# Two transformer blocks on one Trainium2 core: the input x waits in device memory while its on-chip place holds four more buffers of weight parts, and the parts of two tiles are made by one operation

## The chip, the cores and the metric

The program runs on one core of one Trainium2 chip. The core has five engines, each with its own instruction order: TensorE (PE, matrix products), VectorE (DVE), ScalarE (ACT), GpSimd (POOL) and SyncE (SP, which here only issues transfers). They are tied together by semaphores alone: an engine waits until a counter has a value. Sixteen DMA engines move data between device memory (HBM) and the on-chip memory (SBUF, 128 partitions). The metric is the device time of one execution in microseconds (us).

## The reference, cut to what matters

Two blocks follow each other on a sequence of 256 tokens with 2048 features, all in float32. This is the part of each block that the change touches:

```
# block 1
h = rmsnorm(x, pre_mix_norm) * (1 + sc_m) + sh_m
proj = h @ w_in                      # 2048 x 8208: the "first projection"
o_hg  = hgrn2_group(proj[..., :4096])        # gated linear recurrence, 8 heads
o_gdn = gdn_group(proj[..., 4096:])          # convolution + gated delta rule, 8 heads
y = concat([o_hg, o_gdn]) @ w_out
x = x + gt_m * rmsnorm(y, post_mix_norm)     # x is needed again here
...                                          # feed-forward, then block 2:
# block 2, "mixer"
proj = u @ w_in_2                    # q, k, v of four kinds of attention
o = concat([fox, nsa, dilated, differential attention])
y = o @ w_out_2
x = x + ...                                  # and here
```

`x` itself is read before the projection (to normalize it) and after the output product (to add to it). Between those points nothing reads it.

## The kernel before

**Split products.** Each float32 operand of a product is held as two parts: the high part (a copy in the rounded type `fp32r`) and the low part (the operand less its high part). A product is then three: high by high, high by low, low by high. The parts of the activations are made once per phase. The parts of the weights are made on the way: a weight group of 512 rows comes from device memory into a ring of two groups (`core.ring`, `RING = 2`, the tile `weights`), ACT copies a tile of 128 rows into the high half of a buffer (`weight_parts`), DVE subtracts and writes the low half, and PE uses both. `w` has `KG = 4` such buffers of 128 x 2 x 512. A step of this pipeline, one weight tile, is called a *slot*.

**The first projection** (`phase_in_1`) has 256 slots, in 8 turns of 32. A group is four slots; its tiles are two rows of tiles by two chunks of 512 columns, and `place(k)` gives the order: k = 0 and 1 are the first chunk of both rows, k = 2 and 3 the second. Each slot is 12 matmuls: four with the high part alone (L1826), which wait for ACT, then eight (L1833, L1835) behind a wait for DVE. The rules of the pipeline are these:

- ACT may write buffer `slot % 4` once PE is through with slot - 4 (`core.parts_used`, L1981).
- Each half of a group (256 rows) has its own semaphore `core.landed`; ACT waits for half k at k = 0 and 1.
- DVE counts `low_ready` at k = 0 and 1 and `used` at k = 2 and 3. `used` also tells SP that half a ring slot may be loaded anew (`refill`, L104 to L117), so a half is asked for as soon as its two tiles are split.
- At slots 0 and 2 of each turn ACT, after its copy, empties the finished accumulators of the turn before (`empty`, L1855), which needs PE to be at the turn's end.

**What else runs there.** `Pace` ties other work to slots: on each engine, in program order, after the slot's own instruction. For ACT these are activations and convolution taps, for DVE the recurrence (L2056 to L2116) and the sums of the modulation, a product with the weights `w_ada` that DVE does by itself, one `L288` per slot (`pair_ada` from slot 28 on, `ada` from the third turn on). The `w_ada` loads are on SP's queue, in between the refills, and on POOL's in the second half of the first turn. At slot 22 ACT issues the load of the 16 gate columns (L1991); PE's gate products wait for it at slot 34 (semaphore `gates_in`).

**The mixer** (`phase_mixer`) has 224 slots, 14 chunks of 16 tiles, with 256 to 512 columns. Its pipeline is the same (L3187 on ACT, L3435 on DVE, L3049 on PE), with a half of a group being two tiles that follow each other. After its copy for the fourth tile of a chunk ACT empties the accumulators of the chunk before (L3088 to L3098); PE has three banks for them. The four loads of the compression weights `nsa_cmp_w1` are on ACT's queue at slots 18, 23, 28 and 33 (L3078), and PE's compression, paced at slot 40, waits for all of them. After slot 223 the last attention packs still run on PE, ACT and DVE. Between two phases there is a barrier: all engines finish one before any starts the next.

**The other products** (feed-forward, output products) already have pairs: their copy (L1149) and their subtraction (L1229) are 128 x 1024.

`x_t` (`core.xT`, 128 x 16 x 256 float32, 16 KB in each partition, 2048 KB in all) lies in SBUF for the whole program.

## Time and profile before

| | us |
|---|---|
| three runs | 2799.83, 2799.99, 2801.44 |
| their median | 2799.99 |
| the profiled execution | 2793.93 |
| its span in the trace | 2792.2 |

| stage | from, to (us of the span) | what is in it |
|---|---|---|
| setup and first turn | 0 to 140 | modulation, normalized input, slots 0 to 31 |
| first projection | 140 to 549 | slots 32 to 255; slot 48 is multiplied at 178 |
| delta rule (`phase_gdn`) | 549 to 630 | no weights of a projection |
| output product, feed-forward | 630 to 1500 | |
| mixer | 1503 to 1903 | slot 32 is split at 1562, slot 223 multiplied at 1893 |
| output product, SwiGLU, end | 1903 to 2792 | |

A row of the view by line gives the busy time of a group of instructions, the mean time of one, and how long the engine sat idle just before them, with what ended that idle time. PE's rows come in two: PEld is the load of the stationary matrix, PE the multiplication; both may show the same stall. Idle time matters where it is PE's, since PE is the engine that is hardly ever idle.

### The profile page before, as it was taken

Reading aid. Unit: us, or ns where it says so; the run is one execution under the profiler, and the core shown is the slowest. Engines: PE = TensorE matmul, PEld = TensorE weight load, DVE = VectorE, ACT = ScalarE, POOL = GpSimd, SP = SyncE. Lnnn points to the kernel's source line nnn. Section 1 sums busy time; section 2 is a strip of 40 time slices with the busy share of each in tenths; the row PEclk is TensorE's granted clock in tenths of the full one; section 3 lists DMA queues with packets and bytes.
Section 4 is the critical chain, followed back from the end, with each engine's and each line's share of the span. In section 5 each row is a group of like instructions: output and inputs, shape, how many; then the busy total and the mean of one; then the engine's idle time right before and its main releaser. Section 6 shows DMA issues by size and latency. Waiting matters only on the chain. (4 is left out here: it accounts for less than half of the span.)

```text
span 2792.2 us, 49466 instructions
## 1 busy us (share of the span) xinstructions
PE 2668.2 (96%) x18997; PEld 2383.3 (85%) x18997; DVE 1963.2 (70%) x2822; ACT 1412.5 (51%) x2328; POOL 306.2 (11%) x447
## 2 busy tenths in 40 slices
PE   7899999998999999999998999998999999999998
PEld 4679898887878888999998898887878888889998
DVE  2288996687877777898998576656787655555564
ACT  3355757645455555445444555555344444444454
POOL 1011413121011111121221010001011000000000
PEclk9999999999999999999999999999999999999999
DMA  9777676637488888898993765536578655665564
GB/s 370 296 259 238 222 234 196 210 94 244 148 286 271 280 269 272 314 334 304 328 337 127 191 194 155 150 111 221 188 267 292 223 181 180 193 185 187 176 196 133
DMA packets 290166, 632.39 MB, mean 226 GB/s; under 512 B 30722, under 2 KB 51654, under 8 KB 289734
## 3 DMA queue, kind: packets, MB, share of 16 engines
q1 hardware_dynamic: 239120, 484.78, 52.6%
q0 software_dynamic: 39424, 142.62, 14.7%
q10 hardware_dynamic: 11446, 2.54, 0.6%
q8 instruction: 122, 2.00, 0.3%
q14 instruction: 54, 0.44, 0.0%
HBM read 627.77 MB, written 2.10 MB: 226 GB/s over the span
## 5 line engine op out<-in xcount | busy, mean ns | idle before, releaser
L1149 ACT ACTIVATE weight_parts<-weights 128x1024 fp32r<-128x1024 f32 x584 | 607.3, 1057 | 583.8 <-PE accumulators L1340 248.8
L1229 DVE TENSOR_TENSOR weight_parts<-weights,weight_parts 128x1024 fp32r<-128x1024 f32 x584 | 707.8, 1222 | 271.1 <-ACT weight_parts L1149 269.4
L1329 PE MATMUL accumulators<-h_parts,weight_parts 128*128 128x512 f32 x2816 | 780.2, 399 | 22.3 <-DVE h_parts L1216 8.5
L1329 PEld LDWEIGHTS accumulators<-h_parts,weight_parts 128*128 128x128 f32 x2816 | 487.5, 191 | 92.6 <-DVE h_parts L872 10.1
L1340 PEld LDWEIGHTS accumulators<-h_parts,weight_parts 128*128 128x128 f32 x2944 | 454.4, 191 | 72.2 <-DVE weight_parts L1229 10.7
L1340 PE MATMUL accumulators<-h_parts,weight_parts 128*128 128x256 f32 x2944 | 475.1, 283 | 7.7 <-DVE weight_parts L1229 7.7
L1833 PE MATMUL accumulators<-in_h_parts,in_weight_parts 128*128 128x256 f32 x1024 | 264.4, 290 | 20.5 <-DVE in_weight_parts L2142 20.1
L2142 DVE TENSOR_TENSOR in_weight_parts<-weights,in_weight_parts 128x512 fp32r<-128x512 f32 x256 | 186.6, 748 | 110.4 <-ACT in_weight_parts L1983 109.6
L1835 PE MATMUL accumulators<-in_h_parts,in_weight_parts 128*128 128x256 f32 x1024 | 260.7, 286 | 0.0
L1373 PE MATMUL accumulators<-h_parts,weight_parts 128*128 128x512 f32 x864 | 236.5, 395 | 2.0 <-issue 1.8
L1983 ACT ACTIVATE in_weight_parts<-weights 128x512 fp32r<-128x512 f32 x256 | 154.8, 627 | 146.9 <-PE accumulators L1835 101.7
L1833 PEld LDWEIGHTS accumulators<-in_h_parts,in_weight_parts 128*128 128x128 f32 x1024 | 199.4, 195 | 26.4 <-DVE in_weight_parts L2142 25.9
L3049 PE MATMUL accumulators<-in_h_parts,in_weight_parts 128*128 128x256 f32 x1632 | 213.8, 286 | 5.5 <-ACT wide L3098 3.1
L1393 PE MATMUL accumulators<-h_parts,weight_parts 128*128 128x256 f32 x864 | 216.8, 283 | 0.2 <-DVE weight_parts L1229 0.2
L1395 PE MATMUL accumulators<-h_parts,weight_parts 128*128 128x256 f32 x864 | 216.6, 283 | 0.0
L3049 PEld LDWEIGHTS accumulators<-in_h_parts,in_weight_parts 128*128 128x128 f32 x1632 | 201.6, 191 | 15.7 <-issue 8.5
L3435 DVE TENSOR_TENSOR in_weight_parts<-weights,in_weight_parts 128x512 fp32r<-128x512 f32 (+6 forms) x224 | 130.0, 596 | 118.8 <-ACT in_weight_parts L3187 116.9
L1835 PEld LDWEIGHTS accumulators<-in_h_parts,in_weight_parts 128*128 128x128 f32 x1024 | 199.8, 195 | 0.0
L3187 ACT ACTIVATE in_weight_parts<-weights 128x512 fp32r<-128x512 f32 (+6 forms) x224 | 121.2, 554 | 144.7 <-PE accumulators L3049 138.3
L1826 PE MATMUL accumulators<-in_h_parts,in_weight_parts 128*128 128x256 f32 x1024 | 177.7, 296 | 12.7 <-DVE in_h_parts L1661 8.7
L1826 PEld LDWEIGHTS accumulators<-in_h_parts,in_weight_parts 128*128 128x128 f32 x1024 | 142.7, 193 | 41.0 <-issue 22.5
L1373 PEld LDWEIGHTS accumulators<-h_parts,weight_parts 128*128 128x128 f32 x864 | 147.7, 189 | 22.6 <-issue 2.1
(418 smaller groups left out, 3624.7 us busy)
## 6 DMA issues: line engine op xcount, KB each, us to landing
weights<-in_w_ff SPq DMA_DIRECT2D x256, 512.0 KB, 6.0
weights<-in_w_in SPq DMA_DIRECT2D x160, 512.0 KB, 5.3
wide<-in_w_ada SPq DMA_DIRECT2D x112, 512.0 KB, 10.3
h_t<-in_ada_w POOLq DMA_DIRECT2D x112, 512.0 KB, 6.8
weights<-in_ffn_w_gate SPq DMA_DIRECT2D x88, 512.0 KB, 4.5
weights<-in_ffn_w_up SPq DMA_DIRECT2D x88, 512.0 KB, 4.5
weights<-in_ffn_w_down SPq DMA_DIRECT2D x88, 512.0 KB, 4.1
weights<-in_w_out SPq DMA_DIRECT2D x64, 512.0 KB, 5.4
```

The costliest lines, as they stand in the source:

```text
L1149: nc.scalar.activation(w[:, held:held + take, 0, :], core.ring[:, q % RING, k:k + take, :], ACT.Copy).then_inc(core.high_ready, take)
L1229: ins = nc.vector.tensor_tensor(w[:, held:held + take, 1, :], core.ring[:, q % RING, k:k + take, :], w[:, held:held + take, 0, :].bitcast( ...
L1329: nc.tensor.matmul(both(nt), high, x[:, kt].rearrange("p a t -> p (a t)"), start=(kt == 0), stop=False, skip_group_check=True)
L1340: ins = nc.tensor.matmul(rest(nt) if two else acc(c, nt), w[:, held, 1, nt * P:(nt + 1) * P], x[:, kt, 0, :], start=False, stop=(kt == KT ...
L1373: nc.tensor.matmul(both(nt), w[:, held, 0, cols[nt]], xk.rearrange("p a t -> p (a t)"), start=first, stop=False, skip_group_check=True)
L1393: nc.tensor.matmul(accs[nt], w[:, held, 0, cols[nt]], xk[:, 1, :], start=False, stop=False, skip_group_check=True)
L1395: ins = nc.tensor.matmul(accs[nt], w[:, held, 1, cols[nt]], xk[:, 0, :], start=False, stop=(last and nt % 2 == 1), skip_group_check=True)
L1826: nc.tensor.matmul(acc(c, nt), w[:, k, 0, nt * P:(nt + 1) * P], x[:, kt, 0, :], start=(kt == 0 and nt % 2 == 0), stop=False, skip_group_ch ...
L1833: nc.tensor.matmul(acc(c, nt), w[:, k, 0, nt * P:(nt + 1) * P], x[:, kt, 1, :], start=False, stop=False, skip_group_check=True)
L1835: ins = nc.tensor.matmul(acc(c, nt), w[:, k, 1, nt * P:(nt + 1) * P], x[:, kt, 0, :], start=False, stop=(kt == KT - 1 and nt % 2 == 1), sk ...
L2142: ins = nc.vector.tensor_tensor(w[:, k, 1, :], core.ring[:, g % RING, part, :], w[:, k, 0, :].bitcast(F32), ALU.subtract)
L3049: ins = nc.tensor.matmul(out, stationary[:, a], moving[:, b], start=(kt == 0 and i == 0 and j == 0), stop=(kt == KT - 1 and i == 2 and j = ...
```

## The change

The change has four parts.

1. **Pairs.** From slot 48 of the first projection (`DEEP_SLOT`) and slot 32 of the mixer (`MIX_DEEP_SLOT`) on, ACT makes the high parts of two tiles in one operation of 128 x 1024, and DVE the low parts likewise. In the first projection a pair is k = 0, 1 or k = 2, 3: one tile of each half of the group, so ACT waits for both halves before the first pair, and both counts of `used` come with the second pair. In the mixer a pair is a half of a group.
2. **Four more buffers.** From the same slots on, the buffers are eight: the four of `w` and four (`w_in_x`) at the address of `x_t`. ACT waits for PE to be through with slot - 8, of the pair's second tile.
3. **x in device memory.** ACT issues a store of all of `x_t` (2048 KB) to `x_kept` at slot 26 of the first projection and at slot 20 of the mixer. ACT waits for the store's end before it first writes `w_in_x` (slot 52, slot 36). SP loads `x_t` back in the delta-rule phase, and in the mixer after the last matmul that uses a weight part; each of the two phases ends only when that load has landed.
4. **One semaphore** (`gates_in_x_moved`) counts the gate columns and the moves of x. PE's gate products at slot 34 now wait for 32, which is the gate columns and the store of x.

```diff
+X_KEPT_SLOT, DEEP_SLOT = 26, 48
...
+        w_in_x = nc.alloc_sbuf_tensor_at("in_1_weight_parts_in_x", [P, KG, 2, CW], F32R, offset=core.x_at)
...
+        def parts(slot):
+
+            if slot < DEEP_SLOT:
+                return w, slot % KG
+            return (w, slot % (2 * KG)) if slot % (2 * KG) < KG else (w_in_x, slot % (2 * KG) - KG)
+
+        def parts_free(act, slot):
+
+            if DEEP_SLOT + KG <= slot < DEEP_SLOT + 2 * KG:
+                act.wait_ge(core.gates_in_x_moved, 32)
+            elif slot >= KG:
+                act.wait_ge(core.parts_used, slot + 1 - (KG if slot < DEEP_SLOT + KG else 2 * KG))
...
-                pe.wait_ge(s["gates_in"], 16)
+                pe.wait_ge(core.gates_in_x_moved, 32)
...
+                elif k % 2 == 0:
+                    if k == 0:
+                        for half in range(HALVES):
+                            act.wait_ge(core.landed[g % RING][half], 16 * ((st.first + g) // RING + 1))
+                    parts_free(act, slot + 1)
+                    nc.scalar.activation(held[:, at:at + 2, 0, :], core.ring[:, g % RING, part::2, :], ACT.Copy
+                                         ).then_inc(core.high_ready, 2)
...
+                if slot == X_KEPT_SLOT:
+                    act.dma_start(core.x_kept, core.xT[:].rearrange("p a b -> p (a b)")).then_inc(core.gates_in_x_moved, 16)
...
+                elif k % 2 == 0:
+                    dve.wait_ge(core.high_ready, slot + 2)
+                    nc.vector.tensor_tensor(held[:, at:at + 2, 1, :], core.ring[:, g % RING, part::2, :],
+                                            held[:, at:at + 2, 0, :].bitcast(F32), ALU.subtract
+                                            ).then_inc(core.used if k >= 2 else core.low_ready, 2)
...
+        @block.sync
+        def _(sp):
+            sp.dma_start(core.xT[:].rearrange("p a b -> p (a b)"), core.x_kept).then_inc(core.gates_in_x_moved, 16)
+            sp.wait_ge(core.gates_in_x_moved, 48)
...
+MIX_KEPT_SLOT, MIX_DEEP_SLOT = 20, 32
...
             prefetch(sp, core, core.streams["out_2"])
+            sp.wait_ge(core.parts_used, row_tile(0, SLOTS))
+            sp.dma_start(core.xT[:].rearrange("p a b -> p (a b)"), core.x_kept).then_inc(core.gates_in_x_moved, 16)
+            sp.wait_ge(core.gates_in_x_moved, 80)
...
+                    elif k % 2 == 0:
+                        if MIX_DEEP_SLOT + KG <= slot < MIX_DEEP_SLOT + 2 * KG:
+                            act.wait_ge(core.gates_in_x_moved, 64)
+                        else:
+                            back = KG if slot < MIX_DEEP_SLOT + KG else 2 * KG
+                            act.wait_ge(core.parts_used, row_tile(c, kt) + 2 - back)
+                        nc.scalar.activation(held[:, at:at + 2, 0, 0:width], core.ring[:, g % RING, k:k + 2, 0:width],
+                                             ACT.Copy).then_inc(core.high_ready, 2)
```

**DVE, slots 183 to 188 of the first projection.** L2142 (L2175 after) is the subtraction that makes the low parts, L288, L293, L299 and L302 are the modulation's sums, L2080, L2056 and L2061 (L2106, L2082, L2087) the recurrence. Before:

```order
L2142 TENSOR_TENSOR in_1_weight_parts<-weights,in_1_weight_parts 128x512 x2
L288 SCALAR_TENSOR_TENSOR turn_sums<-wide,c_act,turn_sums 128x512
L2056 TENSOR_TENSOR scaled<-h_t 128x1024
L2142 TENSOR_TENSOR in_1_weight_parts<-weights,in_1_weight_parts 128x512
L288 SCALAR_TENSOR_TENSOR turn_sums<-wide,c_act,turn_sums 128x512
L293 TENSOR_TENSOR turn_sums<-turn_sums 128x512
L299 STREAM_TRANSPOSE turn_sums<-turn_sums 128x512
L302 TENSOR_REDUCE modulation<-turn_sums 128x16
L2080 COPY_PREDICATED attn_t<-up_mask,accumulators 64x8x16x2 x2
L2061 TENSOR_TENSOR scaled<-h_t 128x1024
L2142 TENSOR_TENSOR in_1_weight_parts<-weights,in_1_weight_parts 128x512 x5
```

After:

```order
L2175 TENSOR_TENSOR in_1_weight_parts_in_x_49<-weights,in_1_weight_parts_in_x_49 128x2x512
L288 SCALAR_TENSOR_TENSOR turn_sums<-wide,c_act,turn_sums 128x512
L2082 TENSOR_TENSOR scaled<-h_t 128x1024
L2175 TENSOR_TENSOR in_1_weight_parts<-weights,in_1_weight_parts 128x2x512
L288 SCALAR_TENSOR_TENSOR turn_sums<-wide,c_act,turn_sums 128x512
L293 TENSOR_TENSOR turn_sums<-turn_sums 128x512
L299 STREAM_TRANSPOSE turn_sums<-turn_sums 128x512
L302 TENSOR_REDUCE modulation<-turn_sums 128x16
L2106 COPY_PREDICATED attn_t<-up_mask,accumulators 64x8x16x2 x2
L2087 TENSOR_TENSOR scaled<-h_t 128x1024
L2175 TENSOR_TENSOR in_1_weight_parts<-weights,in_1_weight_parts 128x2x512
```

The low part of slot 185 now comes with that of slot 184, ahead of the long run of other work instead of behind it.

**ACT, slots 22 to 28 of the first projection.** L1983 (L2000) is the copy that makes the high parts, L1991 (L2015) the load of the gate columns. Before:

```order
L1991 DMA w_gates<-in_w_in 128x16x16
L1983 ACTIVATE in_1_weight_parts<-weights 128x512 [waits parts_used]
L432 ACTIVATE h_t<-h_t,modulation,affine 128x256 [waits input_factored,input_normalized]
L432 ACTIVATE h_t<-h_t,modulation,affine 128x256 x3
L1656 ACTIVATE in_1_h_parts<-h_t 128x4x256 [waits scalar_steps]
L1983 ACTIVATE in_1_weight_parts<-weights 128x512 [waits parts_used,weights_landed_0_half_0]
L1983 ACTIVATE in_1_weight_parts<-weights 128x512 [waits parts_used,weights_landed_0_half_1]
L1983 ACTIVATE in_1_weight_parts<-weights 128x512 [waits parts_used] x2
L1983 ACTIVATE in_1_weight_parts<-weights 128x512 [waits parts_used,weights_landed_1_half_0]
```

After:

```order
L2015 DMA w_gates<-in_w_in 128x16x16
L2000 ACTIVATE in_1_weight_parts<-weights 128x512 [waits parts_used]
L432 ACTIVATE h_t<-h_t,modulation,affine 128x256 [waits input_factored,input_normalized]
L432 ACTIVATE h_t<-h_t,modulation,affine 128x256 x3
L1658 ACTIVATE in_1_h_parts<-h_t 128x4x256 [waits scalar_steps]
L2000 ACTIVATE in_1_weight_parts<-weights 128x512 [waits parts_used,weights_landed_0_half_0]
L2000 ACTIVATE in_1_weight_parts<-weights 128x512 [waits parts_used,weights_landed_0_half_1]
L2000 ACTIVATE in_1_weight_parts<-weights 128x512 [waits parts_used]
L2018 DMA x_kept<-x_t 128x4096
L2000 ACTIVATE in_1_weight_parts<-weights 128x512 [waits parts_used]
L2000 ACTIVATE in_1_weight_parts<-weights 128x512 [waits parts_used,weights_landed_1_half_0]
```

The store of x stands four copies behind the gate load in the same queue, ahead of the copies of slots 27 and 28.

**SP, the end of the mixer.** The rows are the transfers of the mixer's last weights and of the next product's first ones. Before and after in one piece:

```order
 L117 DMA weights<-in_w_in 128x2x256 x16
 L117 DMA weights<-in_w_out 128x2x512 x4
-L2841 UNCONDITIONAL_BRANCH
+L2924 DMA x_t<-x_kept 128x4096
+L2880 UNCONDITIONAL_BRANCH
```

The load of x is the last thing on SP's queue in the mixer, and the branch to the next phase stands behind it.

## Rows read from the trace of the kernel before

**Rows 1.** The page: busy time of each engine, share of the span, count.
```profile
PE 2668.2 (96%) x18997; PEld 2383.3 (85%) x18997; DVE 1963.2 (70%) x2822; ACT 1412.5 (51%) x2328; POOL 306.2 (11%) x447
```

**Rows 2.** Waits, 178 to 549 us: who waited for whom, total, times, longest.
```profile
PE accumulators L1833 <- DVE in_weight_parts L2142: 18.5, 17, 2.1
...
PEld accumulators L1833 <- DVE in_weight_parts L2142: 24.0, 25, 2.3
...
ACT in_weight_parts L1983 <- PE accumulators L1835: 91.9, 92, 3.7
ACT in_weight_parts L1983 <- DMA weights<-in_w_in: 27.9, 19, 4.1
...
DVE in_weight_parts L2142 <- ACT in_weight_parts L1983: 56.3, 44, 4.3
```

**Rows 3.** Busy time by stretch: length, engines, TensorE clock, DMA share, GB/s.
```profile
178.00:275.00 97.00, 93.61 (x773) 90.53 (x773) 81.64 (x131) 55.15 (x98) 7.87 (x9) 1.00 0.70 226
275.00:297.00 22.00, 19.71 (x144) 18.70 (x143) 22.00 (x25) 14.95 (x29) 15.18 (x12) 0.92 0.69 251
...
326.00:352.00 26.00, 22.00 (x222) 20.99 (x221) 25.64 (x30) 19.12 (x36) 16.39 (x17) 1.00 0.61 207
352.00:402.00 50.00, 48.30 (x482) 47.04 (x482) 44.65 (x66) 31.39 (x51) 5.96 (x7) 1.00 0.77 248
402.00:430.00 28.00, 24.50 (x226) 23.22 (x222) 24.68 (x31) 16.77 (x32) 7.84 (x8) 1.00 0.59 195
...
504.00:527.00 23.00, 20.21 (x157) 18.92 (x156) 22.91 (x30) 15.21 (x20) 0.00 (x0) 1.00 0.65 228
527.00:549.00 22.00, 20.35 (x181) 19.80 (x179) 13.35 (x23) 7.94 (x17) 0.00 (x0) 1.00 0.64 218
```

**Rows 4.** DVE's timeline around slot 185: start, duration, instruction, idle before.
```profile
410.70 0.69 DVE L2142 TENSOR_TENSOR in_weight_parts<-weights,in_weight_parts 128x512 fp32r<-128x512 f32 x1
...
416.94 1.29 DVE L2142 TENSOR_TENSOR in_weight_parts<-weights,in_weight_parts 128x512 fp32r<-128x512 f32 x2
```

**Rows 5.** DVE's timeline at the start of the output product, pairs back to back.
```profile
1905.28 2.35 DVE L1229 TENSOR_TENSOR weight_parts<-weights,weight_parts 128x1024 fp32r<-128x1024 f32 x2
```

**Rows 6.** DMA issues, 178 to 549 us: KB each, median us from issue to landing.
```profile
weights<-in_w_in SPq DMA_DIRECT2D x100, 512.0 KB, 5.3
```

**Rows 7.** ACT's and DVE's timelines, slots 22 to 30.
```profile
115.89 0.40 ACTq L1991 DMA_DIRECT2D w_gates<-in_w_in  x1
...
123.38 2.18 ACT L1983 ACTIVATE in_weight_parts<-weights 128x512 fp32r<-128x512 f32 x4
...
140.03 0.49 DVE L284 TENSOR_SCALAR turn_sums<-wide,c_act 128x512 f32<-128x512 f32 x1 [3.44 <-DMA wide<-in_w_ada]
```

**Rows 8.** Busy time by stretch (as rows 3), and a DMA issue (as rows 6).
```profile
131.00:149.00 18.00, 12.96 (x94) 12.46 (x93) 9.21 (x16) 7.65 (x17) 2.17 (x3) 0.91 0.92 335
...
w_gates<-in_w_in ACTq DMA_DIRECT2D x1, 128.0 KB, 18.0
wide<-in_x SPq DMA_DIRECT2D x1, 2048.0 KB, 7.9
```

**Rows 9.** Waits of PE in the mixer, 1562 to 1894 us (as rows 2).
```profile
PE accumulators L3049 <- DVE in_weight_parts L3435: 5.3, 6, 1.7
PE accumulators L3049 <- ACT wide L3098: 3.8, 5, 1.5
```

**Rows 10.** The mixer's last load on ACT's queue, PE's first use, DMA meanwhile.
```profile
1563.48 0.60 ACTq L3078 DMA_DIRECT2D h_t<-in_nsa_cmp_w  x1
...
1579.29 0.54 PE L2898 MATMUL accumulators<-wide,h_t 128*64 128x30 f32 x12
...
1547.00:1563.00 16.00, 15.40 (x126) 15.28 (x127) 7.44 (x16) 9.29 (x23) 0.00 (x0) 1.00 1.08 243
```

**Rows 11.** PE's timeline at the mixer's end.
```profile
1892.84 0.52 PE L3049 MATMUL accumulators<-in_weight_parts,in_h_parts 128*128 128x256 f32 x3
...
1899.11 2.88 PE L3020 MATMUL accumulators<-maps_t,wide 128*128 128x256 f32 x16 [0.80 <-ACT maps_t L3167]
```

77 lines of the change are left out of this document (51 added, 26 removed).

## The prediction

> **What bounds the kernel now.** I read the page first: PE is busy 96% of the span [rows 1], so only idle time of PE can be won, or matmuls taken away, and the change takes none away. Next came PE's waits where the change works. From slot 48 of the first projection to its end (178 to 549 us) PE waits for DVE's low parts: 18.5 us on the row of the multiplications, 24.0 us on that of the weight loads; these are two views of the same stalls, and the loss lies between [rows 2]. In the mixer it is 5.3 us for low parts and 3.8 us for the emptying of accumulators by ACT [rows 9]. Last, the busy time by stretch, to see why. PE's idle time is the length less PE's busy time: 3.4, 2.3, 4.0, 1.7, 3.5, 2.8 and 1.7 us in the seven stretches of [rows 3], 19.4 us in all. Where it is densest, DVE is busy without a break (22.00 of 22, 25.64 of 26, 22.91 of 23 us). Elsewhere it has time left: over the whole stage it idles 56.3 us waiting for ACT's high parts, and ACT idles 91.9 us waiting for PE to free a buffer [rows 2]. So DVE isn't short of time on average (305.9 of 371 us). It is short of buffers in which to work ahead before a burst of other work. One burst is plain: from 410.70 to 416.94 us DVE makes no low part, since 6 us of modulation sums and recurrence stand between those of slots 184 and 185 [rows 4].
>
> **Part 1, deeper buffers, first projection.** 208 slots take 371 us, 1.8 us each. With four buffers DVE can be ahead by four slots less a copy and a subtraction (0.6 and 0.7 us [rows 4, 7]): 5.9 us at best, 4.5 where slots are short. With eight and pairs it is seven slots less a pair's copy and subtraction (some 1 and 1.2 us [rows 5]), 10 us at best. A burst of 6 us then fits. It fits only if the lead has been earned: DVE must have had idle time first, and at each turn's end ACT must wait for PE's last slots to empty accumulators, which cuts the lead to three slots eight times, in both kernels. So I go by stretch, with DVE's idle time there [rows 3]: 178 to 275 has 15.4 us of it, I take 3.0 of 3.4; 275 to 297 none, 1.2 of 2.3; 326 to 352, 0.4 us, 2.0 of 4.0; 352 to 402, 1.0 of 1.7; 402 to 430, 2.5 of 3.5 (the plain burst, whole, and half of the rest); 504 to 527, 1.2 of 2.8 (it follows a turn's end); 527 to 549, 0.8 of 1.7. That is 11.7 us. In 275 to 297 the granted clock was 0.92, so part of it ran at the lower level, 1.2 GHz instead of 2.4; 0.08 of 22 us is 1.8 us, and it came after PE had stood still. If the stall is half gone I count 0.8 us of that. Sum 12.5 us. The bounds are 3 us (only the first stretch) and 24.0 + 1.8 us.
>
> **Part 2, pairs.** A pair costs 2.35 / 2 = 1.18 us on DVE [rows 5], two singles back to back 1.29 us [rows 4]: 0.11 us saved, 104 times, 11 us of DVE's time. Off the critical path it is worth nothing; in the three stretches without idle time (71 of 371 us, 20 pairs) it is 2.2 us, which is in the sum above. The Trainium skill, "VectorE: DVE Perf Modes", section on the TRN2 errata, says that an operation from SBUF pays a fixed extra latency, about 151 cycles at 0.96 GHz for a float32 subtraction of this kind. By that rule a pair saves 0.16 us, and the dense stretches 3.2 us; the rows of this trace, where operations follow each other without a gap, show less, and I go by them. The price of pairs is in the ring of weights, and it is the first rival.
>
> **Part 3, the mixer.** The same reasoning for its 5.3 us: its bursts are short and its slots too; I take 3.5 us. The 3.8 us is another thing: ACT empties a chunk's accumulators behind its fourth copy, which with four buffers may only start once PE is through with the old chunk. With eight the copy is done before, so the emptying starts one copy (about 0.6 us) earlier; at five recorded waits that is up to 3 us, I take 2.5. Sum 6 us, bounds 1 and 9.1 us.
>
> **Part 4, storing x.** In the first projection the store comes at slot 26. ACT makes the copies of slots 24 to 27 from 123.38 us on, so it is issued at about 125 us, on the queue whose gate load was issued at 115.89 us and took 18.0 us, to 133.9 us [rows 7, 8]. I assume that the store's data follow that. They then fall into 131 to 149 us, when the DMA engines are busy 0.92 of the time at 335 GB/s and PE only 12.96 of 18 us [rows 8]: PE hangs on transfers there, and DVE waits 3.44 us for a `w_ada` load [rows 7]. 2.1 MB at 335 GB/s are 6.3 us. If all of it goes ahead of what PE needs, PE loses 6.3 us; if it goes between, nothing. PE's gate products at slot 34 (about 148 us) now also wait for the store. Shared with two other queues at a third of the rate the store takes 6.3 x 3 = 19 us, to 153 us, but PE will be late by then itself. The delays overlap, so I take 3.5 us for both; bounds 0 and 6.3. What is queued on PE behind the gates' wait is slot 35's matmuls, so the wait is paid in full if it occurs. In the mixer the store goes between the first and second of four loads for the compression. The last of these is issued at 1563.48 us, PE first uses them at 1579.29 us, and DMA is at 1.08 meanwhile [rows 10]. A delay of up to 2.1 MB / 243 GB/s = 8.6 us falls on a cover of 15.8 us less a landing of some 6 to 10 us. I take 1.5 us, bounds 0 and 8.6. Both issues on ACT (0.4 to 0.6 us each, by the other loads there) are covered by its lead.
>
> **Part 5, loading x back.** In the delta-rule phase it is issued first and has 81 us; nothing there waits for it, so nothing, as long as it lands within the phase. At the mixer's end it decides: it starts when the last weight matmul is over (1893.4 us), a 2048 KB load took 7.9 us [rows 8], so it lands at 1901.3 us; the mixer's last matmul ends at 1902.0 us [rows 11]. The cover is 0.7 us. The first weights of the output product stand ahead in the same queue; if 1 MB of them is still on the way, 3.1 us at 335 GB/s come on top: 2.4 us late. I take 1.0, bounds 0 and 2.4.
>
> **The sum.** 12.5 + 6 - 3.5 - 1.5 - 1.0 = 12.5 us less. From the profiled execution's 2793.93 us that gives 2781.4; the median of the runs is 6.06 us above it, so 2787.5 us. I say **2787 us**.
>
> **Rivals.** *The ring of weights takes the place of the buffers.* It still holds two groups. In the first projection both halves are now given back with the second pair, and both must have landed before the first copy. Between DVE's end of one group and its start on the next but one lies one group of work, 4 x 1.8 = 7.1 us; needed are 5.3 us of landing [rows 6] and a copy of 1 us, 6.3 us. On average it fits, with 0.8 us to spare; where slots are 1.5 us it doesn't (6.0 us), and ACT has waited 27.9 us for weights already [rows 2]. Then the lead is never earned and part 1 gives 4 us instead of 12.5: 2796 us. *DMA time decides (slower).* Store and load cost their bounds, 6.3 + 8.6 + 2.4 = 17.3 us, and the weights come later too, so that parts 1 and 3 give 4 + 6. That is 7 us more: 2807 us. It decides from the point at which x costs more than the 10 us left. For it speaks DMA at 0.92 and 1.08 just where the stores fall, against it the 0.6 to 0.7 in most of [rows 3]. "DMA: Bandwidth & Descriptors" in the Trainium skill, section on issuing engines, says that transfers from all queues end on the same 16 engines and interleave. By that x's own queue buys nothing, which leans to this rival; no row here has three queues at once. *Nearly all stalls go.* The lead of ten microseconds covers every burst: 19.4 + 1.8 + 9.1 - 6 = 24 us less, 2776 us. For it speaks that no single recorded stall is longer than 2.1 us [rows 2], against it the turns' ends.
>
> **How the numbers follow.** Forecast 0.55 (own range 2780 to 2794), ring 0.20, DMA 0.10, nearly all 0.15. About 0.2%, 5.6 us, is what a measurement can tell from no change. Faster by more than that (under 2794.4) are the forecast, nearly all, and a tenth of the ring's case: 0.72. Slower (over 2805.6): 0.11. The same: 0.17. The range holds the forecast, the ring's case and most of nearly all, and leaves out DMA and the best cases: 2770 to 2803.
>
> **What would show it.** In the profile after, PE's wait for DVE's low parts in the first projection should fall from 18.5 to about 7 us, and DVE should still be without a break in the dense stretches. If ACT's wait for weights rises well over 27.9 us and its wait for PE falls to little, it was the ring. If slot 48 is multiplied more than 5 us later than at 178 us, or the mixer's last phase ends behind x's landing, it was DMA. A new wait of PE at the gate or compression products shows part 4. The prediction is wrong if the lead of DVE doesn't grow past four slots, or if the moves of x cost over 10 us.

## The result: slower by 0.6%

The changed kernel takes 2813.72 us (median of 10 runs, 2807.65 to 2822.76); the kernel before, run beside it, takes 2798.84 us (10 runs, 2790.51 to 2802.09). The ratio is 1.0061, with a 95% interval of 1.0049 to 1.0073: slower by 15 to 17 us, where 12.5 us less were forecast, and outside the range. The profiled execution after is the slowest of its ten, 2822.76 us with a span of 2820.8 us, and the profiled execution before (2793.93 us) is one of the shorter ones. The two traces are therefore 28.8 us apart where the medians are 14.9 apart: the sizes of whole kernels are taken from the medians, and the traces say where the time goes, in sizes that run too high in all.

Where the time goes is read by laying the two traces over each other: for each slot of the first projection the start of its first matmul after, less that before, and for the mixer the same at every 96th matmul. The lag in us:

```
first projection, slot   0    28    32    48    64    112   160   208   255
after - before         +1.5  +1.4  +8.2  +8.2  +6.9 +13.0 +15.9 +23.4 +27.4
mixer, at (before)      1521  1565  1594  1664  1743  1893 us
after - before         +31.6 +32.4 +34.7 +32.1 +31.6 +28.4
```

There are three pieces: a step of 6.8 us between slots 28 and 32, a growth of 19.3 us from slot 48 to 255, and in the mixer a step of 3.3 us followed by a gain of 6.3 us. The 4.2 us between the two stages are put down to the execution and not to the change; in the runs below that same stretch varies from -7 to +6 us.

**The growth behind slot 48.** The waits of the changed kernel from 178 to 570 us, beside [rows 2] (engine, tile and line, who released it, total us, times, longest):

```profile
ACT in_weight_parts L2007 <- DMA weights<-in_w_in: 52.2, 12, 8.4
DVE in_weight_parts L2175 <- ACT in_weight_parts L2007: 48.4, 22, 5.7
ACT in_weight_parts_in_x L2007 <- DMA weights<-in_w_in: 46.0, 12, 6.7
DVE in_weight_parts_in_x L2175 <- ACT in_weight_parts_in_x L2007: 43.0, 20, 3.5
...
ACT in_weight_parts L2007 <- PE accumulators L1851: 20.2, 5, 6.1
...
PE accumulators L1849 <- DVE in_weight_parts_in_x L2175: 11.1, 13, 1.8
PE accumulators L1849 <- DVE in_weight_parts L2175: 11.0, 10, 3.1
...
ACT in_weight_parts_in_x L2007 <- PE accumulators L1851: 4.9, 3, 2.5
```

Each wait now stands on two rows, for the old and the new buffers. ACT's wait for PE's buffers fell from 91.9 to 25.1 us, as the deeper buffers promise, but its wait for weights rose from 27.9 to 98.2 us, and DVE's wait for ACT from 56.3 to 91.4 us. PE's wait for DVE went from 18.5 to 22.1 us instead of to 7. The same in the dense stretches (busy time in each window; length, PE, PEld, DVE, ACT, POOL, TensorE clock, DMA share, GB/s):

```profile
285.00:308.00 23.00, 18.25 (x143) 17.14 (x142) 18.74 (x19) 14.20 (x23) 13.71 (x12) 1.00 0.63 223
337.00:365.00 28.00, 22.03 (x190) 20.66 (x189) 24.05 (x24) 18.71 (x30) 16.73 (x16) 0.97 0.56 189
```

DVE, which had no break there [rows 3], now idles 4.3 of 23 and 4.0 of 28 us, and PE stands still for 4.8 and 6.0 us, longer than before. The DMA engines are busy only 0.56 to 0.63 of the time, so it isn't their bandwidth: the weights are asked for too late (which runs without the coupling, below, bear out).

**The step at slot 32.** DVE's timeline after, beside [rows 7] (start, duration, line, in brackets idle before and its releaser), the same window as [rows 8], and the transfers from 120 to 150 us (KB each, median us to landing):

```profile
146.28 0.49 DVE L284 TENSOR_SCALAR turn_sums<-wide,c_act 128x512 f32<-128x512 f32 x1 [8.30 <-DMA wide<-in_w_ada]
...
131.00:149.00 18.00, 8.37 (x46) 7.39 (x45) 3.15 (x6) 3.25 (x7) 0.72 (x1) 0.78 0.85 344
...
wide<-in_w_ada POOLq DMA_DIRECT2D x5, 512.0 KB, 22.2
weights<-in_w_in SPq DMA_DIRECT2D x4, 512.0 KB, 17.9
x_kept<-x_t ACTq DMA_DIRECT2D x1, 2048.0 KB, 22.0
```

DVE waits 8.30 us for the first modulation load where it waited 3.44. It works in order, so its next low parts wait behind that sum; PE is busy 8.37 us of 18 instead of 12.96, and the granted clock falls from 0.91 to 0.78. The new wait of PE for the store, at the gate products, costs nothing: the lag is 8.2 us at slot 32 and at slot 48, the store has landed at 146.0 us, and the first gate product starts at 157.7 us.

### The profile page after: what moved, and what is told of

It is laid out like the page before. It is cut to its first block and busy times, and to the rows that moved or that the text cites. A ratio compares the mean times of both kernels' runs of the same rounds, so it can differ in the third digit from the quotient of the medians.

```text
span 2820.8 us, 49227 instructions
## 1 busy us (share of the span) xinstructions
PE 2677.9 (95%) x18997; PEld 2389.4 (85%) x18997; DVE 1936.5 (69%) x2622; ACT 1375.0 (49%) x2128; POOL 310.9 (11%) x447
## 5 line engine op out<-in xcount | busy, mean ns | idle before, releaser
L1329 PEld LDWEIGHTS accumulators<-h_parts,weight_parts 128*128 128x128 f32 x2816 | 486.1, 191 | 96.2 <-DVE h_parts L872 10.1
L1340 PEld LDWEIGHTS accumulators<-h_parts,weight_parts 128*128 128x128 f32 x2944 | 453.2, 190 | 70.3 <-DVE weight_parts L1229 10.1
L1340 PE MATMUL accumulators<-h_parts,weight_parts 128*128 128x256 f32 x2944 | 473.7, 283 | 6.7 <-DVE weight_parts L1229 6.5
L1393 PE MATMUL accumulators<-h_parts,weight_parts 128*128 128x256 f32 x864 | 216.7, 283 | 0.4 <-DVE weight_parts L1229 0.4
L1395 PE MATMUL accumulators<-h_parts,weight_parts 128*128 128x256 f32 x864 | 216.6, 283 | 0.0
L1849 PE MATMUL accumulators<-in_h_parts,in_weight_parts 128*128 128x256 f32 x608 | 163.1, 298 | 17.2 <-DVE in_weight_parts L2175 11.0
L1373 PEld LDWEIGHTS accumulators<-h_parts,weight_parts 128*128 128x128 f32 x864 | 147.7, 189 | 23.4 <-issue 2.1
L1393 PEld LDWEIGHTS accumulators<-h_parts,weight_parts 128*128 128x128 f32 x864 | 165.9, 192 | 0.6 <-DVE weight_parts L1229 0.6
L1395 PEld LDWEIGHTS accumulators<-h_parts,weight_parts 128*128 128x128 f32 x864 | 165.9, 192 | 0.0
L288 DVE SCALAR_TENSOR_TENSOR ada_sums<-h_t,c_act,ada_sums 128x512 f32<-128x512 f32 x224 | 159.9, 746 | 3.1 <-DMA h_t<-in_ada_w 2.8
L1851 PE MATMUL accumulators<-in_h_parts,in_weight_parts 128*128 128x256 f32 x608 | 160.9, 294 | 0.0
L238 POOL DMA_DIRECT2D h_t<-in_ada_w x112 | 80.5, 719 | 724.3 <-DVE ada_sums L288 237.7
L1376 PEld LDWEIGHTS accumulators<-h_parts,weight_parts 128*128 128x128 f32 x864 | 132.5, 189 | 18.4
L1849 PEld LDWEIGHTS accumulators<-in_h_parts,in_weight_parts 128*128 128x128 f32 x608 | 123.1, 203 | 20.4 <-DVE in_weight_parts L2175 13.7
L1389 PE MATMUL accumulators<-h_parts,weight_parts 128*128 128x256 f32 x864 | 138.9, 283 | 0.0
L1148 ACT ACTIVATE h_parts<-wide 128x512 fp32r<-128x512 f32 x108 | 68.6, 636 | 141.3 <-DMA weights<-in_w_ff 59.6
L1376 PE MATMUL accumulators<-h_parts,weight_parts 128*128 128x256 f32 x864 | 137.4, 281 | 0.0
L1842 PE MATMUL accumulators<-in_h_parts,in_weight_parts 128*128 128x256 f32 x608 | 108.7, 302 | 18.2 <-DVE in_h_parts L1663 10.0
```

The source lines that it names most:

```text
L288: ins = nc.vector.scalar_tensor_tensor(out=acc, in0=w, scalar=number, in1=acc, op0=ALU.mult, op1=ALU.add)
L1329: nc.tensor.matmul(both(nt), high, x[:, kt].rearrange("p a t -> p (a t)"), start=(kt == 0), stop=False, skip_group_check=True)
L1340: ins = nc.tensor.matmul(rest(nt) if two else acc(c, nt), w[:, held, 1, nt * P:(nt + 1) * P], x[:, kt, 0, :], start=False, stop=(kt == KT ...
L1373: nc.tensor.matmul(both(nt), w[:, held, 0, cols[nt]], xk.rearrange("p a t -> p (a t)"), start=first, stop=False, skip_group_check=True)
L1376: ins = nc.tensor.matmul(rest(nt), w[:, held, 1, cols[nt]], xk[:, 0, :], start=False, stop=last, skip_group_check=True)
L1389: nc.tensor.matmul(accs[nt], w[:, held, 0, cols[nt]], xk[:, 0, :], start=(first and nt % 2 == 0), stop=False, skip_group_check=True)
```

## The experiments

Two theories about the growth were put against each other: **A**, the ring of weights is coupled (a pair takes one tile of either half, so both halves are wanted at the first copy and given back at the last), and **C**, operations of two tiles cost by themselves. **B** puts the whole loss on the moves of x. All medians below are beside 2795.56 us for the kernel before (19 to 22 runs beside them), those of before_light, deep_light, mixer_only and late_mix_pairs beside 2795.13 us (31 runs), and the last two beside 2795.78 us (17 runs).

**x_moves_only**: the change without its buffers and pairs, in both stages (the diff is the first projection's).

```diff
-            if slot < DEEP_SLOT:
+            if True:
                 return w, slot % KG
...
-                if slot < DEEP_SLOT:
+                if True:
                     if k < HALVES:
```

> The two stores and two loads of x and the shared semaphore of the change, and nothing else of it: four buffers and one tile per operation, as before. Theory A (from slot 48 on the pairs, which take a tile of each half of a group, hold both halves until the second pair and want both before the first copy, so that the weights in the ring become the limit; the store of x costs about 7 us at slots 30 to 40, the other moves 2 to 4): 2806 to 2811 us where the kernel before has 2799, that is +7 to +12, with the whole loss of the first projection in place by slot 48. Theory B (the store and the loads of x are the whole slowdown, by what they do to later transfers): +15 to +17, with the lag still growing after slot 48. Theory C (operations of two tiles are the cost by themselves): as A.

Measured: 2806.95 us, ratio 1.0038 (1.0027 to 1.0050), +11.4 us. The lag steps by 6.5 us at slot 32, stays at 6.7 until slot 136, ends at 8.9, and steps by 2.9 us in the mixer at 1577 us. So the moves of x cost 11 us by themselves, all but 2 us of the traced part in two steps; B falls as the whole, since the growth behind slot 48 is missing.

**deep_single**: the change, eight buffers and moves of x, with one tile per operation.

```diff
-                if slot < DEEP_SLOT:
+                if True:
                     if k < HALVES:
                         act.wait_ge(core.landed[g % RING][k], 16 * ((st.first + g) // RING + 1))
```

> The changed kernel with one tile per operation in both stages; the eight buffers and the moves of x stay. Theory A: the halves of a group are again wanted and given back one at a time, so the lag behind the kernel before stops growing at slot 48 and the deeper buffers win some of it back: 2794 to 2806 us (-5 to +7). Theory B (moves of x): as the changed kernel, +15. Theory C (operations of two tiles cost by themselves): as A. Theory D (eight buffers themselves are harmful, because refills are asked for in other places and collide): +10 or more, with growing lag.

Measured: 2794.73 us, ratio 0.9996 (0.9986 to 1.0005). The pairs are therefore worth some 16 to 19 us of loss (each kernel's median beside its own kernel before gives 15.7 us, the ratios 1.0061 and 0.9996, 0.65% apart, give 18.2 us, the two medians 19.0 us; the intervals leave 4 us to either side), as much as the whole slowdown. From 178 to 570 us ACT's waits read:

```profile
ACT in_weight_parts L2000 <- DMA weights<-in_w_in: 46.1, 24, 5.8
ACT in_weight_parts_in_x L2000 <- DMA weights<-in_w_in: 37.0, 21, 4.6
...
PE accumulators L1849 <- DVE in_weight_parts L2170: 12.9, 11, 2.1
...
PE accumulators L1849 <- DVE in_weight_parts_in_x L2170: 7.0, 9, 1.4
```

Here too ACT waits for weights (83.1 us) in place of buffers, but PE's wait for DVE is 19.9 us, as it was. The first projection from slot 48 to 255 loses 0.8 us in this trace and gains nothing. Against x_moves_only the kernel is 12.2 us faster by the medians and 8.2 us by the two profiled executions; the traces place 1.5 us of that in the first projection and 5.3 us by the mixer's end, and more runs below were made to tell whether the first projection has a share.

**pairs_four**: pairs as in the change, four buffers, no move of x.

```diff
-            if slot < DEEP_SLOT:
+            if True:
                 return w, slot % KG
...
-                if slot == X_KEPT_SLOT:
-                    act.dma_start(core.x_kept, core.xT[:].rearrange("p a b -> p (a b)")).then_inc(core.gates_in_x_moved, 16)
```

> Operations of two tiles as in the change, with four buffers only and without any move of x. Theory A: the ring coupled, and no depth: the lag grows from slot 48 by at least the 19 us that the changed kernel loses there, and perhaps by twice that as TensorE now waits for pairs: +20 to +45 us in all, ScalarE waiting over 70 us for weights in the first projection. Theory B (moves of x): no change or a gain, -5 to +3. Theory C: as A.

Measured: 2840.82 us, ratio 1.0157 (1.0133 to 1.0181), +45 us, at the upper end of A's range. The lag is 0 at slot 48, 30.7 us at slot 255, and grows by 15.9 us through the mixer, where a pair lies in one half and nothing is coupled. With four buffers, then, pairs have a second cost: only two operations' worth of buffers are left, and ACT waits 127.1 us for PE (91.9 before). The deep buffers pay for that part. ScalarE's wait for weights, though, is 31.9 us and not the 70 that A had named: with four buffers the longer wait is that for buffers.

**halves_coupled**: the kernel before, single tiles, four buffers, and only the coupling, from slot 48 on (so the second hunk too).

```diff
-                if k < HALVES:
-                    act.wait_ge(core.landed[g % RING][k], 16 * ((st.first + g) // RING + 1))
+                if k == 0:
+                    for half in range(HALVES if slot >= 48 else 1):
+                        act.wait_ge(core.landed[g % RING][half], 16 * ((st.first + g) // RING + 1))
...
-                ins.then_inc(core.used if k >= 2 else core.low_ready, 1)
+                ins.then_inc(core.used if k == 3 else core.low_ready, 2 if k == 3 else 1)
```

> The kernel before with one tile per operation and four buffers, but from slot 48 of the first projection on ScalarE waits for both halves of a group ahead of its first copy and VectorE gives both back after its fourth remainder. Nothing else. This is the coupling alone. Theory A: +12 to +30 us, all of it in the first projection behind slot 48, ScalarE's waits for weights going from 28 us to over 70. Theory C (it is the two-tile operations themselves, not the coupling): within 4 us of the kernel before. Theory B: the same.

Measured: 2808.78 us, ratio 1.0049 (1.0032 to 1.0066), +13.2 us, and in the trace 14.1 us from slot 48 to 255. ACT's row, beside 27.9 in [rows 2]:

```profile
ACT in_weight_parts L1988 <- DMA weights<-in_w_in: 78.5, 28, 5.4
ACT in_weight_parts L1988 <- PE accumulators L1837: 51.1, 48, 5.1
```

No operation has changed its size here; the coupling alone costs 13 us (n is four; the interval leaves 9 to 18). It has two parts, the wait for both halves and their late return, and no run tells these apart.

**deep_coupled**: deep_single with that same coupling, so that only its size of operation differs from the change.

```diff
+                    if k == 0:
+                        for half in range(HALVES if slot >= DEEP_SLOT else 1):
+                            act.wait_ge(core.landed[g % RING][half], 16 * ((st.first + g) // RING + 1))
...
-                                            ).then_inc(core.used if k >= 2 else core.low_ready, 1)
+                                            ).then_inc(core.used if k == 3 else core.low_ready, 2 if k == 3 else 1)
```

> One tile per operation, eight buffers and the moves of x (the kernel deep_single, 2795 us), and from slot 48 of the first projection on both halves of a group awaited at its first copy and given back with its fourth remainder. Theory A (the coupling of the halves is what the two-tile operations cost): most of the 17 us that lie between deep_single and the changed kernel, +11 to +18 over deep_single: 2806 to 2813 us, with ScalarE's waits for weights near the 98 us of the changed kernel. Theory C (the size of the operations costs, since TensorE can start only when both tiles are copied and subtracted): within 4 us of deep_single, 2791 to 2799.

Measured: 2810.97 us, ratio 1.0052 (1.0036 to 1.0069), 16.2 us over deep_single; slot 48 to 255 grows by 15.5 us (19.3 in the changed kernel). ACT idles 112 us ahead of its copies from 178 to 570 us (A had said near 98), though its rows name no releaser there. A holds; the remainder of some 2 us is within what the intervals leave open.

**rows_pairs**: the change with its pairs inside one half of a group, that is the two chunks of one row tile.

```diff
-        return k // 2, k % 2, 2 * (k % 2) + k // 2
+        if slot >= DEEP_SLOT:
+            return k % 2, k // 2, k
+        return k // 2, k % 2, 2 * (k % 2) + k // 2
...
-                        for half in range(HALVES):
-                            act.wait_ge(core.landed[g % RING][half], 16 * ((st.first + g) // RING + 1))
+                    act.wait_ge(core.landed[g % RING][k // 2], 16 * ((st.first + g) // RING + 1))
```

> The changed kernel with its two-tile operations, but from slot 48 of the first projection on in the other order: a pair is the two tiles of one half (the two chunks of one row tile), awaits that half alone and gives it back at once; the second chunk's accumulators are emptied a slot earlier to fit. Theory A: the 17 us over deep_single go, and with fewer operations perhaps 1 to 3 us more: 2790 to 2798 us. Theory C (size of the operations): 2808 to 2814, as the changed kernel.

Measured: 2803.15 us, ratio 1.0033 (1.0020 to 1.0047): 8 us over deep_single, and by the ratios 0.28% or 8 us under the change. Neither theory's range holds it. Undoing the coupling gives back half. The other half is lost from slot 48 to 255 (8.4 us in the trace). Three things stayed or came with the new order: the size of the operations, the emptying of the second chunk at another slot, and SP's queue. A half is now given back a slot or two sooner, but modulation loads that wait for DVE stand ahead of its refill (SP's waits from 178 to 550 us):

```profile
SPq L238 <- DVE turn_sums L288: 159.3, 42, 8.2
SPq L117 <- DVE in_weight_parts L2179: 83.1, 26, 9.8
SPq L117 <- DVE in_weight_parts_in_x L2179: 57.5, 28, 4.7
```

Summed over the 104 refills of that part, 129 us pass between DVE's last low part of a half and the issue of its refill, 24 us in deep_single. The last two kernels below were made to tell the three apart.

**deep_late**: deep_single with both stores of x moved. The store in the first projection also waits on ACT for the gate columns to have landed, PE's gate products no longer wait for it, and the mixer's deep buffers start at slot 56.

```diff
-X_KEPT_SLOT, DEEP_SLOT = 26, 48
+X_KEPT_SLOT, DEEP_SLOT = 36, 48
...
-MIX_KEPT_SLOT, MIX_DEEP_SLOT = 20, 32
+MIX_KEPT_SLOT, MIX_DEEP_SLOT = 42, 56
...
-                pe.wait_ge(core.gates_in_x_moved, 32)
+                pe.wait_ge(core.gates_in_x_moved, 16)
```

> deep_single (2795 us) with both stores of x moved: in the first projection from slot 26 to slot 36, behind the chip's last use of the modulation loads of slots 28 to 32, and the gate columns' product waiting for its own load alone; in the mixer from slot 20 to slot 42, behind the loads of W1, with the deep buffers from slot 56 instead of 32. Theory E (a store at slot 26 and 20 costs what it does because it collides with loads that somebody is about to want: 6.7 and 2.9 us in the traces): 2785 to 2789 us. Theory F (2 MB cost their DMA time wherever they stand): within 3 us of deep_single, 2792 to 2798.

Measured: 2790.27 us, ratio 0.9982 (0.9972 to 0.9991), 4.5 us under deep_single and 5.3 us under the kernel before. Both steps are gone: the lag is 1.3 and 1.2 us at slots 28 and 32 (0.2 and 6.5 in deep_single), and in the mixer -1.88 us at 1565 and at 1594 us. The window of [rows 8] and the store, issued at 148.7 us, read:

```profile
131.00:149.00 18.00, 12.96 (x93) 12.27 (x93) 8.01 (x14) 7.29 (x17) 1.83 (x3) 0.90 0.85 305
...
x_kept<-x_t ACTq DMA_DIRECT2D x1, 2048.0 KB, 10.6
```

PE's 12.96 us are back to the digit, and the store lands in 10.6 instead of 22.0 us. E holds: the place of the store costs, not its bytes. (That PE's gate products no longer wait for the store can't be the reason, since deep_single's step lies ahead of slot 34.) The time is a microsecond above E's range.

**rows_late**: rows_pairs and the moved stores together.

> rows_pairs and the moved stores of deep_late together. Theories A and E: 2781 to 2788 us, faster than both kernels. If A holds and F instead of E: 2790 to 2798. If C holds: over 2800 whichever of E and F does.

Measured: 2793.78 us, ratio 0.9987 (0.9977 to 0.9997), 3.5 us over deep_late. The moved stores give 9.4 us here, the two traced steps together; the trace still grows by 7.7 us from slot 48 to 255. The time lies in none of the ranges for A and E together (up to 2788) or for C (over 2800); it is in the one for F, but deep_late has ruled F out.

**before_light** and **deep_light**: the kernel before, and deep_late, with refills that bring half of the columns.

```diff
+        if stream is core.streams["in_1"] and stream.unit * i + q >= 14:
+            cols = cols // 2
+        sp.dma_start(ring[:, slot, at, 0:cols], src[:, at, 0:cols]).then_inc(core.landed[slot][half], 16)
```

> The kernel before with the refills of the first projection from group 14 on (slot 56) bringing half of each tile's columns only; the other half of the columns in the ring is what lay there, so this leaves out half of the weights' transfers and no work of the engines. It asks what weights that land sooner are worth with four buffers. Theory G (with four buffers ScalarE waits for the buffers that TensorE gives back, 92 us against 28 us for weights, so sooner weights do little): 0 to -4 us, 2791 to 2796.

> deep_late (eight buffers, one tile per operation, stores of x moved; 2790 us) with the same half-sized refills from group 14 of the first projection on. Theory G (with eight buffers the ring of weights has taken the buffers' place, ScalarE waiting 88 us for weights): the lead is now earned, -8 to -15 us against deep_late: 2775 to 2782, and ScalarE's waits for weights fall under 30 us. Theory H (VectorE's own work in the dense stretches is the limit, and earlier weights only move waits about): within 3 us of deep_late, 2787 to 2793.

Measured: before_light 2792.76 us, ratio 0.9990 (0.9981 to 0.9999), deep_light 2789.36 us, ratio 0.9980 (0.9970 to 0.9989). The refill of deep_light lands in 3.6 us instead of 5.0:

```profile
weights<-in_w_in SPq DMA_DIRECT2D x70, 256.0 KB, 3.6
```

and yet it is only 0.9 us under deep_late. G falls and H's range holds: once the halves are uncoupled, weights that land sooner buy next to nothing. ACT's wait for them falls from 88.1 to 60.7 us (G had it under 30), so the ring isn't out of play yet, and a longer ring wasn't tried; but those 27 us less bought 0.9. How full the buffers really were answers why. Counted in the traces, for each of the 208 slots from 48 on: how many slots' low parts were ready when PE started the slot, its own included (0 means that its own isn't ready yet).

```
kernel        mean ready   slots with 0 / 1 / 2 / 3 / 4 / 5 ready
before           1.35        48 / 71 / 57 / 32 /  0 /  0
deep_late        1.54        48 / 67 / 45 / 32 / 13 /  3
deep_light       1.70        48 / 62 / 39 / 29 / 23 /  7
after            1.68        34 / 71 / 59 / 24 / 11 /  9
```

With four buffers DVE stood at its limit of three in 32 slots of 208, and in 48 it had nothing ready. With eight those 48 are still 48, and 42 of them are the same slots, slot 185 behind the plain burst of [rows 4] among them. They come in 23 runs in the kernel before; only in 1 of these had the buffers been full within the four slots ahead, and in 7 within eight. The buffers were full just where they weren't needed. (In the changed kernel PE finds its slot unready less often, 34 times, and yet loses more: its longest recorded wait for low parts is 3.1 us instead of 2.1, and it now waits 4.6 us for high parts, 0.6 before.)

**mixer_only**: the first projection as before, the change in the mixer with the store at slot 42 and deep buffers from slot 56. **late_mix_pairs**: deep_late with the change's pairs in the mixer.

```diff
-MIX_KEPT_SLOT, MIX_DEEP_SLOT = 20, 32
+MIX_KEPT_SLOT, MIX_DEEP_SLOT = 42, 56
...
-                if slot < DEEP_SLOT:
+                if True:
                     if k < HALVES:
```

> The first projection as in the kernel before; in the attention stage the change's eight buffers and two-tile operations, with the store of x at slot 42 and the deep buffers from slot 56. If the first projection's part brings nothing even with its store moved, and the mixer's part 3.5 to 4.5 us as in the traces of deep_late and rows_late: 2790 to 2793 us where the kernel before has 2795.6, that is -3 to -5. If the first projection's deep buffers bring something of their own, this is worse than deep_late (2790) by that much.

> deep_late with the change's two-tile operations in the attention stage, where a pair lies in one half of a group. From the traces a pair there wins 0.7 (rows_late against deep_late) to 2.8 us (the changed kernel against deep_single): 2787.5 to 2789.5 us. If operations of two tiles cost by themselves there too: over 2791.

Measured: mixer_only 2790.07 us, ratio 0.9982 (0.9971 to 0.9992); late_mix_pairs 2789.44 us, ratio 0.9978 (0.9969 to 0.9987), the fastest of those that load all of the weights and 5.7 us under the kernel before. From the mixer's 480th matmul to its end the lag changes by -5.7 and -5.6 us in the two, by -3.6 in deep_late with single tiles. The mixer's part is therefore the whole gain as far as these runs can tell, and the eight buffers of the first projection are worth nothing that they show: late_mix_pairs has them and mixer_only hasn't, and the intervals of the two leave 3 us of loss to 5 us of gain. That pairs beat single tiles in the mixer is what most traces show (by some 2 us, in rows_late by 0.7 only); the medians (0.8 us) can't tell it.

**rows_single**: rows_late with one tile per operation in the first projection, its order of slots kept.

```diff
-                    nc.scalar.activation(held[:, at:at + 2, 0, :], core.ring[:, g % RING, part:part + 2, :], ACT.Copy
-                                         ).then_inc(core.high_ready, 2)
+                    nc.scalar.activation(held[:, at, 0, :], core.ring[:, g % RING, part, :], ACT.Copy
+                                         ).then_inc(core.high_ready, 1)
```

> rows_late (2793.8 us) with one tile per operation in the first projection, but its order of slots (both chunks of a row tile, a half given back with its second tile) and its earlier emptying of the second chunk kept. If the size of the operations is what rows_late loses against deep_late (2790.3), this comes out as deep_late with pairs in the mixer, 2788.5 to 2791 us, and the 7.7 us of growth from slot 48 to 255 go. If the order of the slots, the queue of refills or the emptying is the cause: 2793 to 2796 us, with the growth kept.

Measured: 2797.98 us, ratio 1.0006 (0.9997 to 1.0015). The growth from slot 48 to 255 is still there, 7.8 us, with no operation of two tiles left in that stage, so the size of the operations isn't what rows_late and rows_pairs lose; if anything it wins (0.9987 against 1.0006, intervals that just touch). C falls. The loss comes with the order of the slots. It isn't SP's queue either as far as this run goes, since the 104 refills are 61.5 us late in sum here and 129 in rows_late, with the same growth. In rows_late and rows_single it comes in steps, one of the largest (3.0 and 3.5 us) right behind slot 64, where a turn starts and the first accumulators are emptied at the new slots. PE waits there for that emptying, 2.1 us in rows_late and 2.6 in rows_single, a wait that deep_late lacks:

```profile
PE accumulators L1844 <- ACT wide L1877: 3.6, 2, 2.6
```

That is rows_single from 178 to 570 us; in rows_late the same row is 2.5 us. So the emptying accounts for a third to a half of the 7.8 us, and the rest stays open.

**rows_loads_later**: rows_late with each modulation load one refill later in the queue.

```diff
-AFTER_REFILL = {2: (2, 3), 3: (4,), 4: (5,), 5: (6, 7), 6: (8,), 7: (9,)}
-BEHIND_PAIR = {7: (8, 9)}
+AFTER_REFILL = {0: (1,), 3: (2, 3), 4: (4,), 5: (5,), 6: (6, 7), 7: (8,)}
+BEHIND_PAIR = {7: (8,)}
```

> rows_late with the first projection's modulation loads issued one refill later in the queue that they share with the refills, so that fewer refills stand behind a load that waits for VectorE. If the queue is the cause: 2787 to 2791 us and the 129 us summed over 104 refills between a half's return and the issue of its refill fall under 60. If the size of the operations is the cause: within 2 us of rows_late, 2792 to 2796, whatever the refills do.

Measured: 2828.46 us, ratio 1.0108 (1.0090 to 1.0126), 35 us over rows_late, which neither expectation had. The refills did what was meant, 5.9 us late in the sum of 104 instead of 129. But the modulation loads have no slack either:

```profile
DVE turn_sums L288 <- DMA wide<-in_w_ada: 49.4, 20, 4.5
```

In [rows 2] no such wait is among the large ones. DVE works in order, so the low parts behind each such sum wait too, and the queue's order is already a compromise between the two. What refills in time are worth by themselves this run can't tell.

## Why the prediction was wrong, point by point

**What bounds the kernel.** Right as to the rows, wrong in the reading "it is short of buffers in which to work ahead". The evidence was ACT's wait of 91.9 us for PE to free a buffer. That wait says that ACT was far ahead, not that DVE was held up: in 32 of 208 slots DVE had filled what there was, and only 1 of the 23 runs of unready slots came within four slots of such a place. The stalls fall where DVE had been behind for longer, and buffers that DVE hasn't filled before are no help there.

**Part 1, deeper buffers, first projection (12.5 us).** This is one of the two steps that failed; the other, the larger, is the price of the pairs in part 2. The text named its condition, "only if the lead has been earned", and then counted DVE's idle time in a stretch as earned lead. Measured without the pairs: 0.8 us lost in deep_single, 0.4 gained in deep_late, and 2.5 with weights that land in 3.6 us. All of these are within what executions differ by: mixer_only, whose first projection is that of the kernel before, loses 3.1 us in the same stretch. So the 12.5 us became nothing that the runs can tell, at most some 5. With the change's pairs it is 19.3 us lost in the trace. The lower bound of 3 us was no bound either: a loss had been left out. The sign named for a wrong prediction, a lead that doesn't grow past four slots, nearly came: five slots were ready in 3 of 208 slots in deep_late and in 9 in the changed kernel, never more, where seven had been counted on.

**Part 2, pairs, and the first rival.** The mechanism was named exactly: both halves wanted before the first copy and given back with the second pair. ACT's wait for weights "well over 27.9 us" with little wait for PE was the sign given, and it came (98.2 and 25.1 us). Its size was wrong: 6.3 us needed against 7.1 us there "on average" was taken to fit, leaving 4 us of gain (2796 us). An average of 0.8 us to spare isn't slack when slots, averaged over eight, take from 1.4 us (168 to 176) to 2.5 us (208 to 216) in the kernel before. That a group that comes late also delays its own return, and so the next group but one, is the likely reason for the size and not shown. The coupling costs 13.2 us with four buffers and 16.2 with eight. In the sum the pairs' price stood at nothing, and it is this term, not part 1, that turned no gain into a loss: with parts 1 and 2 at nothing and the rest as measured the kernel would be about 5 us slower, not 15. That pairs are worth nothing "off the critical path" was right; they are worth less than nothing where they tie two transfers together. Their size alone does no harm (rows_single).

**Part 3, the mixer (6 us).** Right in the sum: from 1594 us to its end the changed kernel gains 6.3 us, rows_pairs 6.3, late_mix_pairs 5.6. The two terms behind it were off in opposite directions, though. PE's waits behind the store, from 1597 to 1894 us before (the first two rows; that for the low parts is the first of [rows 9]) and from 1631 to 1923 us after (the other four), where L3088 and L3098 (L3138 and L3148) are the emptying:

```profile
PE accumulators L3049 <- ACT wide L3098: 3.2, 4, 1.5
PE accumulators L3049 <- ACT wide L3088: 1.2, 2, 0.8
...
PE accumulators L3099 <- DVE in_weight_parts L3506: 2.9, 2, 1.7
PE accumulators L3099 <- DVE in_weight_parts_in_x L3506: 1.1, 1, 1.1
PE accumulators L3099 <- ACT wide L3148: 0.3, 1, 0.3
PE accumulators L3099 <- ACT wide L3138: 0.2, 1, 0.2
```

The low parts' 5.3 us fell by 1.3 and not by 3.5, and in deep_late they didn't fall at all (5.3 us from 1594 to 1888 us); the emptying gave 3.9 us and not 2.5. The last microsecond of the 6.3 is on none of these rows. So here too the lead brought little, and it was luck that the other term made up for it.

**Part 4, the stores (3.5 and 1.5 us).** The place and the way were right, the sizes too small. The first cost 6.8 us (6.5 in x_moves_only), above the upper bound of 6.3. That bound was the store's own bytes at 335 GB/s; it left out that DVE waits in order, so that one late modulation load stops the low parts too, and that PE, once still, runs on at a lower clock (0.78 for 0.91). The store doesn't merely follow the gate load on its own queue: the modulation loads and the refills land late with it, 22.2 and 17.9 us after their issue. Nor did it take "a third of the rate". The queues from 137 to 142 us of the changed kernel (q10 is ACT's, q0 POOL's, q1 SP's: packets, MB, share of the 16 DMA engines' time):

```profile
q10 hardware_dynamic: 88, 1.44, 67.7%
q0 software_dynamic: 87, 0.36, 17.3%
q1 hardware_dynamic: 90, 0.33, 16.0%
```

The three queues get equally many packets, but one of the store's is 16 KB (a row of `x_t` in a partition) and one of the others 4 KB or less, so the store takes two thirds of the bytes while DVE waits for a load on q0. The second cost 3.3 us against 1.5, inside its bounds. It stands in the same trouble, beside the compression's loads and refills that land in 8.5 us instead of 7.1 (transfers issued from 1575 to 1600 us; 7.1 is that of 1545 to 1570 us before; no landing recorded for the second row):

```profile
weights<-in_w_in SPq DMA_DIRECT2D x5, 512.0 KB, 8.5
h_t<-in_nsa_cmp_w ACTq DMA_DIRECT2D x4, 512.0 KB
x_kept<-x_t ACTq DMA_DIRECT2D x1, 2048.0 KB, 10.0
```

By "DMA: Bandwidth & Descriptors" in the Trainium skill, section on issuing engines, transfers of all queues end on the same 16 engines and interleave; the trace now shows three queues at once and agrees, with 373 to 486 GB/s in all from 134.25 to 147 us and packets of all three in turn.

**Part 5, loading back (0 and 1.0 us).** Right. The first load, issued at 577.5 us, lands in 8.4 us, within its phase, and nothing waits for it. The second is issued at 1921.8 us; its landing (first row) and PE's timeline behind the mixer's last matmul (second) read:

```profile
x_t<-x_kept SPq DMA_DIRECT2D x1, 2048.0 KB, 10.0
...
1934.71 2.07 PE L1329 MATMUL accumulators<-h_parts,weight_parts 128*128 128x512 f32 x4 [4.29 <-DVE h_parts L1216]
```

The wait of 4.29 us was 3.42 us before. In x_moves_only, deep_single and deep_late the load lands in 7.7 us and the wait is 3.42 us, so there it is hidden; in late_mix_pairs it lands in 9.5 us and the wait is 3.77. In the changed kernel, with 10.0 us, it puts 0.9 us on the path, by the forecast's way and nearly its size.

**The sum.** In the medians: the moves of x 11.4 us for the 6.0 forecast; the deeper buffers with single tiles -12.2 us for both stages, where parts 1 and 3 had -18.5; the pairs 16 to 19 us, where the sum had nothing. These are differences from one kernel to the next, so they add up to the 15 to 17 us measured by construction, and say how the loss divides and no more. Of the -12.2 us the traces place only part (3.6 to 4.2 us in the mixer, 1.5 in the first projection); the rest isn't placed, and the interval of that difference is 4 us to either side. The rival that ended slower (2807 us, chance 0.10) named the wrong mechanism for most of it, though its sign came (slot 48 is multiplied 8.2 us later); the ring's rival had the right one and the wrong sign. They were added up as alternatives, though both could, and did, happen at once.

## What to carry to other kernels

An engine's wait for free buffers shows that it is ahead, not that the engine behind it lacks buffers; before deepening them, count how often they are full shortly ahead of a stall. An operation of two tiles should take two that arrive together and leave together, since otherwise it makes a ring of two groups into a ring of one. A transfer that nobody waits for still has to be put where nobody's transfer is about to be waited for: ten slots later (22 in the mixer), the same two megabytes cost nothing that the traces show.

## What the runs showed of the hardware

The 128 KB load of the gate columns, in pieces of 64 bytes, does more than take 18.0 us itself [rows 8]. In the changed kernel, from 120 us to 132 us the DMA engines move 3 to 13 GB/s in all, while the modulation loads (issued from 125.5 us on another queue), refills and the store (124.0 us) are waiting; only then do they rise to 400 GB/s. The busy tenths and GB/s of 120 to 150 us in 40 slices:

```profile
DMA  0000001110000000135999999999999999999759
GB/s 8 7 7 7 8 9 13 12 12 8 8 7 7 5 3 6 40 124 197 373 459 393 486 382 399 475 399 475 382 388 426 399 421 410 410 415 366 279 213 202
```

From 118 to 131 us all 1680 packets (0.11 MB) are those of ACT's queue, which holds this load. That it is what holds the others back is read from this order of events and wasn't tried in a run of its own. If it is, the kernel before pays for it too: there DVE waits 8.69 us, up to 135.90 us, for ACT's copy of weights that land late, and then the 3.44 us for the modulation load. The other thing is how much a stretch varies from one execution to the next: the lag between the end of the first projection and the start of the mixer changes by -7.1 us (halves_coupled) to +5.8 us (mixer_only), in two kernels that have no edit there, so that a difference of 5 us between two traces has to be found in its own stage, or in the medians.
